# Taking every third weighted sum of the first tile's rounds from TensorE to ScalarE and GpSimd

## The reference

```python
def peer_block(x, wq, k1, k2, U, V):
    ...
    e = (...)                                   # 8 heads x 16 experts of 16384, for each token
    g = jax.nn.softmax(sc, axis=-1)
    act = jax.nn.gelu(jnp.einsum('nd,nhjd->nhj', x, U[e]), approximate=False)
    out = jnp.einsum('nhj,nhjd->nd', g * act, V[e])
    return out.astype(x.dtype)
```

## Time and profile before

| what | value |
|---|---|
| median of 3 runs | 2743.24 us (2741.44 to 2760.86) |
| the profiled execution | 2737.79 us, its span from first to last instruction 2735.9 us |
| busy, share of the span | PE 84%, DVE 53%, ACT 15%, POOL 14% |
| mean granted TensorE clock | 0.941 of full speed |
| gathers | 320, 671.11 MB, 58.3% of the 16 DMA engines' span |
| first gather issued, last gather issued | 1027.1 us, 2704.1 us |
| time in which POOL sat idle ahead of a gather until TensorE had summed a row | 1301.0 us, 311 times |
| time in which DVE sat idle ahead of a dot until a gather had landed | 521.2 us |

### The profile page before, as it was taken

How to read it: one execution, slowest core, us unless ns; L and a number is a source line. 1 busy time by engine, 2 the same in 40 slices (tenths; PEclk the granted TensorE clock), 3 DMA queues, 4 the chain that set the end, 5 groups by cost and what they waited for, 6 DMA issues and landing times.

```text
span 2735.9 us, 21188 instructions
## 1 busy us (share of the span) xinstructions
PE 2301.7 (84%) x7673; PEld 1264.8 (46%) x7673; DVE 1458.5 (53%) x2651; ACT 417.9 (15%) x879; POOL 379.7 (14%) x363
## 2 busy tenths in 40 slices
PE   4999999785689898999899999877877777777776
PEld 3999999543555343434344444322322232222221
DVE  4333333465620015656754455888888865555554
ACT  3222222321310010011200001211111100010000
POOL 0000000000010001221212222222222122222221
PEclk8999999866589899999999999999999999999999
DMA  4444443214035879999999999999999999999997
GB/s 128 148 128 134 142 151 119 76 56 114 1 119 183 287 264 408 418 373 426 389 421 425 416 404 420 413 415 421 407 414 422 424 417 428 428 428 428 428 429 298
DMA packets 159866, 844.78 MB, mean 309 GB/s; under 512 B 9862, under 2 KB 97730, under 8 KB 117274
## 3 DMA queue, kind: packets, MB, share of 16 engines
q0 software_dynamic: 46080, 671.11, 58.3%
q1 hardware_dynamic: 113706, 172.67, 19.0%
HBM read 833.26 MB, written 10.21 MB: 308 GB/s over the span
## 4 chain that ended last, share of the span: by engine, by line
PE 56%; DMA 27%; DVE 11%; issue 4%; ACT 1%; SPq 0%; DVEq 0%; POOL 0%; ACTq 0%; POOLq 0%
DMA rows_in<-in_peer_uv,expert 26%; PE bank L246 19%; PE bank L272 7%; PE bank L1025 5%; PE bank L1026 5%; PE bank L1027 5%; PE bank L259 4%; DVE rows_in L548 3%; PE bank L1002 1%; PE bank L1217 1%; PE bank L1207 1%; PE bank L1179 1%; DVE diag L523 1%; PE bank L1143 1%; PE bank L1132 1%
## 5 line engine op out<-in xcount | busy, mean ns | idle before, releaser
L246 PE MATMUL bank<-rows_in,diag 128*128 128x512 f32 (+1 forms) x2560 | 1189.0, 611 | 268.7 <-DVE diag L523 268.1
L548 DVE CUSTOM_DVE_ANT_0 rows_in<-rows_in,x2n 128x2048 f32<-128x2048 f32 x320 | 733.5, 2292 | 521.7 <-DMA rows_in<-in_peer_uv,expert 521.2
L246 PEld LDWEIGHTS bank<-rows_in,diag 128*128 128x128 f32 (+1 forms) x2560 | 451.9, 183 | 987.3 <-issue 546.0
L454 POOL DMA_INDIRECT rows_in<-in_peer_uv,expert x320 | 364.5, 1139 | 1509.4 <-PE bank L246 1301.0
L1025 PE MATMUL bank<-xnh,wh 128*128 128x336 f32 x896 | 285.8, 319 | 23.2 <-DVE wl L1448 23.2
L356 ACT ACTIVATE dots<-dots 128x1 f32<-128x1 f32 x320 | 64.9, 203 | 1507.8 <-DVE dots L548 1507.8
L1027 PE MATMUL bank<-xnh,wl 128*128 128x336 f32 x896 | 286.0, 319 | 0.0
L1026 PE MATMUL bank<-xnl,wh 128*128 128x336 f32 x896 | 285.6, 319 | 0.0
L1448 DVE TENSOR_TENSOR wl<-wring,wh 128x2048 fp32r<-128x2048 f32 x56 | 128.2, 2292 | 266.1 <-ACT wh L1271 266.1
L1025 PEld LDWEIGHTS bank<-xnh,wh 128*128 128x128 f32 x896 | 170.6, 190 | 24.0 <-issue 24.0
L1026 PEld LDWEIGHTS bank<-xnl,wh 128*128 128x128 f32 x896 | 170.5, 190 | 0.0
(11 more groups left out here) (288 smaller groups left out, 1517.3 us busy)
## 6 DMA issues: line engine op xcount, KB each, us to landing
wring<-in_w_in SPq DMA_DIRECT2D x28, 2048.0 KB, 8.2
wk<-in_w_out SPq DMA_DIRECT2D x64, 512.0 KB, 9.1
wk<-in_peer_wq SPq DMA_DIRECT2D x64, 512.0 KB, 8.7
kT<-in_keys_t SPq DMA_DIRECT2D x16, 512.0 KB, 5.5
vpage<-in_cache_v SPq DMA_DIRECT2D x16, 512.0 KB
rows_in<-in_peer_uv,expert POOLq DMA_INDIRECT x320, 12.4
C<-in_state_C SPq DMA_DIRECT2D x4, 1024.0 KB, 5.8
out_C_sample<-C SPq DMA_DIRECT2D x4, 1024.0 KB, 4.5
```

Source lines behind the costliest of these rows:

```text
L246: mm = pe.matmul(accs[t][d][0:w, :], diag[r % ND][:, 0:w], rows_in[r % NG][:, D + 512 * d:D + 512 * d + 512], start=False, stop=(j == ROUN ...
L454: nc.gpsimd.indirect_dma_start(out=rows_in[r % NG][:], out_offset=None, in_=UV_DR, in_offset=bass.IndirectOffsetOnAxis(ap=ids[:, j:j + 1], ...
L548: nc.vector.tensor_tensor_reduce(u, u, x2n[t][:], 1.0, 0.0, ALU.mult, ALU.add, dots[t % 2][:, j:j + 1]).then_inc(S["dot_done"], 1)
```

## The change

Of tile 0's 128 rounds, those with r % 3 == 2 (2, 5, ..., 125, which are 42) no longer go through TensorE. ScalarE multiplies the dot's gelu with the gate, and then the V half of the gathered row, in place, with that number. GpSimd adds the scaled row to `h1[0]`, ahead of the gather that reuses the buffer (that of round r+4), and waits for its own add before it issues that gather. No diagonal is built for those rounds. The residual `h1[0]` now carries a part of the sum, so TensorE adds it by the identity behind tile 0's last round and not ahead of its first. VectorE signals each finished gate (`gate_ready`). The counts that stand behind `acc_done` are renumbered.

```diff
--- before.py
+++ after.py
@@ -172,6 +172,25 @@
     FIRST = [0, PH * PK, 2 * PH * PK]
     TOTAL = sum(ROUNDS)
     COLS = [P, P, TS]
+    OWN = 3
+
+    def on_pool(r):
+
+        return r < FIRST[1] and r % OWN == OWN - 1
+
+    def pool_sums(r):
+
+        return sum(1 for n in range(r) if on_pool(n))
+
+    def tensor_sums(r):
+
+        return r - pool_sums(r)
+
+    def tensor_steps(r):
+
+        return tensor_sums(r) + (1 if r >= FIRST[1] else 0)
+
+    TILE_STEPS = [tensor_sums(FIRST[1]) + 1, tensor_sums(FIRST[2]) + 1, tensor_sums(TOTAL) + 1]
 
     def tile_of(r):
 
@@ -233,19 +252,27 @@
 
             t, j = tile_of(r)
             w = COLS[t]
-            if j == 0:
+            if on_pool(r):
+                return
+            if j == 0 and t:
                 if t == 1:
                     banks_idle(pe, ("pS", 2, 3), range(4))
                 elif t == 2:
                     pe.wait_ge(S["y_done"], 1)
                 for d in range(4):
                     pe.matmul(accs[t][d][0:w, :], ident[:, 0:w], h1[t][:, 512 * d:512 * d + 512], start=True, stop=False, skip_group_check=True)
-            pe.wait_ge(S["diag_done"], r + 1)
+            n = tensor_sums(r)
+            pe.wait_ge(S["diag_done"], n + 1)
             pe.wait_ge(row_in[r % NG], 16 * (r // NG + 1))
             for d in range(4):
-                mm = pe.matmul(accs[t][d][0:w, :], diag[r % ND][:, 0:w], rows_in[r % NG][:, D + 512 * d:D + 512 * d + 512],
-                               start=False, stop=(j == ROUNDS[t] - 1), skip_group_check=True)
+                mm = pe.matmul(accs[t][d][0:w, :], diag[n % ND][:, 0:w], rows_in[r % NG][:, D + 512 * d:D + 512 * d + 512],
+                               start=(r == 0), stop=(t > 0 and j == ROUNDS[t] - 1), skip_group_check=True)
             mm.then_inc(S["acc_done"], 1)
+            if r == FIRST[1] - 1:
+                pe.wait_ge(S["own_done"], pool_sums(FIRST[1]))
+                for d in range(4):
+                    mm = pe.matmul(accs[0][d][:], ident, h1[0][:, 512 * d:512 * d + 512], start=False, stop=True, skip_group_check=True)
+                mm.then_inc(S["acc_done"], 1)
 
         def product(part, lhs, beside):
 
@@ -338,7 +365,7 @@
         def row_squares(t):
 
             w = COLS[t]
-            act.wait_ge(S["acc_done"], FIRST[t] + ROUNDS[t])
+            act.wait_ge(S["acc_done"], TILE_STEPS[t])
             for d in range(4):
                 ins = nc.scalar.activation(h1[t][0:w, 512 * d:512 * d + 512], accs[t][d][0:w, :], ACT.Square, accum_out=ssq[0:w, d:d + 1])
             ins.then_inc(S["sums_sq"], 1)
@@ -354,6 +381,12 @@
             t, j = tile_of(r)
             act.wait_ge(S["dot_done"], r + 1)
             nc.scalar.activation(dots[t % 2][:, j:j + 1], dots[t % 2][:, j:j + 1], ACT.Gelu).then_inc(S["gelu_done"], 1)
+            if on_pool(r):
+                act.wait_ge(S["gate_ready"], j // PK + 1)
+                act.wait_ge(S["gelu_done"], r + 1)
+                link(nc.scalar.mul(dots[0][:, j:j + 1], dots[0][:, j:j + 1], gate[0][:, j // PK, j % PK:j % PK + 1]))
+                v = rows_in[r % NG][:, D:2 * D]
+                nc.scalar.mul(v, v, dots[0][:, j:j + 1]).then_inc(S["scaled"], 1)
             if t and j == 0:
                 row_squares(t - 1)
             if t and j == 1:
@@ -450,7 +483,13 @@
                 if t < 2 and j % PK == 0:
                     pool.wait_ge(S["e_done"], PH * t + j // PK + 1)
                 if r >= NG:
-                    pool.wait_ge(S["acc_done"], r - NG + 1)
+                    if on_pool(r - NG):
+                        n = pool_sums(r - NG) + 1
+                        pool.wait_ge(S["scaled"], n)
+                        nc.gpsimd.tensor_tensor(h1[0][:], h1[0][:], rows_in[(r - NG) % NG][:, D:2 * D], ALU.add).then_inc(S["own_done"], 1)
+                        pool.wait_ge(S["own_done"], n)
+                    else:
+                        pool.wait_ge(S["acc_done"], tensor_steps(r - NG) + 1)
                 nc.gpsimd.indirect_dma_start(out=rows_in[r % NG][:], out_offset=None, in_=UV_DR,
                                              in_offset=bass.IndirectOffsetOnAxis(ap=ids[:, j:j + 1], axis=0)).then_inc(row_in[r % NG], 16)
 
@@ -500,7 +539,9 @@
                 nc.vector.scalar_tensor_tensor(expert[t][:, PK * h:PK * h + PK], slot[:, 0, :], float(NK), slot[:, 1, :], ALU.mult, ALU.add).then_inc(S["e_done"], 1)
                 dve.wait_ge(S["gate_exp"], PH * t + h + 1)
                 link(nc.vector.reciprocal(gsum[t][:, h:h + 1], gsum[t][:, h:h + 1]))
-                link(nc.vector.tensor_scalar(gate[t][:, h, :], gate[t][:, h, :], gsum[t][:, h:h + 1], None, ALU.mult))
+                ins = nc.vector.tensor_scalar(gate[t][:, h, :], gate[t][:, h, :], gsum[t][:, h:h + 1], None, ALU.mult)
+                ins.then_inc(S["gate_ready"], 1)
+                dve.wait_ge(S["gate_ready"], PH * t + h + 1)
 
         def halves():
 
@@ -518,9 +559,12 @@
             weight = gate[t][:].rearrange("p h k -> p (h k)") if t < 2 else gate2[:]
             src = ident if t < 2 else ident2[:]
             dve.wait_ge(S["gelu_done"], r + 1)
-            if r >= ND:
-                dve.wait_ge(S["acc_done"], r - ND + 1)
-            nc.vector.tensor_scalar(diag[r % ND][:, 0:COLS[t]], src, dots[t % 2][:, j:j + 1], weight[:, j:j + 1], ALU.mult, ALU.mult).then_inc(S["diag_done"], 1)
+            n = tensor_sums(r)
+            if on_pool(r):
+                return
+            if n >= ND:
+                dve.wait_ge(S["acc_done"], n - ND + 1 + (1 if n - ND >= tensor_sums(FIRST[1]) else 0))
+            nc.vector.tensor_scalar(diag[n % ND][:, 0:COLS[t]], src, dots[t % 2][:, j:j + 1], weight[:, j:j + 1], ALU.mult, ALU.mult).then_inc(S["diag_done"], 1)
 
         def row_mean(t):
 
@@ -807,7 +851,7 @@
             "qpad_zero", "qpad_done", "k_in0", "k_in1", "v_in0", "v_in1", "logitS_done", "expS_done", "probS_done",
             "best_done", "gate_exp", "e_done", "wk_used", "xr_in", "g2_in", "keys_in", "norm_sq", "norm_ms", "norm_rms",
             "x2n_done", "mix_dup", "c_rows",
-            "dot_done", "gelu_done", "diag_done", "acc_done", "sums_sq", "sums_ms", "sums_rms", "y_done", "gf_in",
+            "own_done", "scaled", "gate_ready", "dot_done", "gelu_done", "diag_done", "acc_done", "sums_sq", "sums_ms", "sums_rms", "y_done", "gf_in",
         )}
 
         row_in = [sem(f"row_in{n}") for n in range(NG)]
```

## The result

The changed kernel takes 2800.34 us (median of 4 runs, 2795.64 to 2805.65). The four runs of the kernel before that were taken beside it have a median of 2751.87 us, 48 us less. The ratio is 1.0187, with a 95% interval of 1.0154 to 1.022: clearly slower, by 1.5 to 2.2%. I had forecast 2739 us with a range of 2720 to 2768. The ratio of e2_write_only leaves out one of its ten executions, which took 10798 us for no known reason, where the others took 2734 to 2754.

A forecast was written before the change was run, and what follows sets the result against it. DMA and PE were both taken to bound tile 0's rounds beside the projections, DMA alone from 1700 on. Two shallower dips gave -2.6 - 1.5 = -4.1, so 2743.2 - 4 = 2739 us, range 2720 to 2768.

The forecast's parts named there:

- The bound: Tile 0's rounds beside the projections: PE 17.2 us and DMA 17.1 us for three rounds and two k-steps, both bounding.
- the ceiling: From 1050 to 1700, at most what DMA loses at 411 GB/s against 428: 26 us.
- my 4.1: Forecast gain in tile 0's rounds: 2.6 us from the first dip and 1.5 us from the second.
- The first dip: DMA share low from 1180 to 1192: gather 27 issued at 1178.8, not 1186.8; 2 of 4.6 us idle stay.
- The scaling: ScalarE's multiplication of the gathered row, priced at 1.91 us as the cast of 128 x 2048.
- The addition: GpSimd's addition of 128 x 2048, priced at 4.3 us from a copy of 64 columns, between 1.8 and 8.5.
- The step that failed: Row behind a GpSimd row: its dot starts 3.5 us late, so it needs 10.2 us, still inside 13.2.
- The 6.7: A TensorE row's time from landing to next issue: dot, gelu, diagonal and round, 6.7 us.
- my terms: A TensorE row's parts: 2.29 + 0.1 (dot), 0.2 (gelu), 0.3 + 0.4 (diagonal), 3.43 (round).
- a limit of 13.2: Four buffers at 5.7 us a round give 22.9 us; less 9.7 for a gather, 13.2 from landing to issue.
- The addition is slow and holds the next dot: Rival, row behind a GpSimd row: additions from 7.3 us on exceed 13.2; at 8.5, +48 us, 2791; chance 0.14.
- its rival: TensorE's clock falls with gaps in its work, deciding only from 0.80 down; at 0.75, +46 us, 2789; chance 0.08.

The follow-up runs named there:

- e2_write_only: Changed kernel with each GpSimd addition replaced by two memsets of the used buffer: 759.3 us from gather 0 to gather 136 (the stage), ratio to before 1.000.
- e13_no_add_late_dot: Changed kernel without GpSimd's additions, VectorE reducing 3500 columns ahead of 32 dots behind GpSimd rows: 794.9 us from gather 0 to gather 136, ratio to before 1.0113.

## Why the prediction was wrong

**The bound and the ceiling held.** DMA and TensorE both bound the stage. TensorE's saving brought nothing by itself; with the additions taken away the stage gained 4.5 us (7.5 without scaling) against my 4.1 and a ceiling of 26. That 4.5 and 4.1 are so near is luck: 11 us were gained, of which I had 4.1, and 7 lost, of which I had none.

**The first dip went as described.** In the changed kernel gather 27 is issued 25.7 us behind gather 23, where it was 33.1; I had 25.1. Without additions it is 22.0 us, and gather 28 follows 37.4 us behind gather 23 (33.3 in the changed kernel) against 36.2 forecast. The dip is shallower; stretches of the run without additions:

```profile
1201.00:1207.00 6.00, 6.00 (x16) 2.65 (x15) 4.13 (x9) 2.50 (x3) 0.89 (x1) 1.00 0.79 314
1207.00:1213.00 6.00, 6.00 (x16) 2.65 (x15) 3.68 (x11) 0.20 (x1) 1.93 (x3) 1.00 0.88 344
```

That is (0.21 + 0.12) x 6 = 2.0 us idle, where the earlier trace rows give 4.6. I had said that 2 us would stay.

**The prices.** The scaling: 1.91 forecast, 2.00 measured. The addition: 4.3 forecast, 4.54 on average (4.50 undisturbed). The figure of the Trainium skill, 4497 ns (GPSIMD Engine Reference, section 3.1), was nearer. The row that my price came from, a copy of 64 columns, was a poor ground: a long copy takes 1.89 us, so my slope was twice too steep, and it came out near the truth by luck, as an addition takes over twice as long as a copy.

**The step that failed** is "If GpSimd and VectorE shut each other out, that dot starts 3.5 us late and its row needs 6.7 + 3.5 = 10.2 us, still inside 13.2." The exclusion was foreseen, with its place and its size (115 us over 31 dots, 3.7 each). What was wrong is the row's path around it and the slack that I tested it against: a delay of 3.8 us alone, with GpSimd doing nothing but issue gathers, already cost 35 us in e13_no_add_late_dot. The 6.7 was too small from the start. From the end of a dot to the gather into its buffer my terms have 0.2 + 0.3 + 0.4 + 3.43 = 4.3 us. In the timelines it is, on average over the 36 rows behind a GpSimd row from round 12 to round 119, 7.9 us in the kernel before, 6.6 without additions and 8.1 in the changed kernel. There these rows take 13.8 us on average from landing to issue, and up to 21.5, where I had 10.2 against a limit of 13.2.

One row shows the terms. The one that lands at 1455.9 has its dot until 1462.0 (6.1 us, 5.9 by my terms), the diagonal until 1462.7, then TensorE's round, which I had at 3.43. It takes 8.85 - 3.43 = 5.4 us: TensorE had been idle for 5 us, and its clock was granted at 0.68 and 0.76 in these microseconds; then 0.26 for the hand-over. The gather into this buffer is issued at 1468.4, 12.5 us after the landing, and its issue takes 2.49 and not 0.94 us, as it waits for the next dot. The effective time is 12.5 + 1.55 = 14.1 us against 13.2. Two smaller errors go the same way. The 13.2 us were for rounds of 5.7 us; with the projections gone a round is due each 4.9, the loop is 19.6 us, and the margin shrinks by 3.3 us: there each addition cost 2.3 us in place of 1.1. And I tested each buffer alone against its limit, when the delay of one dot is handed to the row behind it, which waits for the same VectorE and the same TensorE. How much of the loss each of these terms makes is not shown; no run takes one of them away alone. The slow issues aren't needed for it: the run with late dots has only 26 of 132 over 1.5 us (25 before) and lost 35 us.

**The rival.** "The addition is slow and holds the next dot" was the right mechanism with a wrong threshold. I let it decide from 7.3 us on, and it decides between 2.35 and 4.5 us (768.0 and 818.3 us in the stage). My 48 us for it were near the measured 54 by luck, for an addition of 8.5 us. TensorE's clock fell from 0.99 to 0.90 as its rival had it, and didn't decide by itself: at 0.93 the run without additions lost nothing over the stage. It has a part in the slow restart above; how much of the loss that is, and whether it makes the 7 us that this run loses behind gather 104, stays open.

## What to carry to other kernels

In these runs VectorE and GpSimd behaved as one engine wherever both read SBUF. So before work is moved to the idle one of the two, look at what the other does in the same microseconds, and price the mover's whole length as a delay of it, on dots, diagonals and short helpers alike. When such a delay is checked against the slack of a ring of buffers, read the path itself from the trace and don't add it up from its parts, add the terms that only appear once things are late (a matmul that starts after idleness, an issue that waits in its turn), and take the ring's shortest period, not its usual one. And ask first what can be won: here 42 rows taken away for almost nothing brought 7.5 us of 2740.

## What the runs showed of the hardware that I had not expected

- The exclusion works in both directions: an addition that comes just behind a dot's start takes 6.6 us in place of 4.5. And it works on the issue of an indirect DMA: 0.94 us undisturbed, 2.7 us beside a dot, ending 0.8 us after it. With VectorE's long sums 60 of the first 132 issues took over 1.5 us, and in the kernel before already 25.
- A GpSimd copy with one input holds dots back as an addition does (dots of up to 4.70 us); GpSimd memsets don't, but they hold the diagonals, a `tensor_scalar` of 128 columns, which then take up to 4.1 us in place of 0.35.
- Cutting GpSimd's instruction in four doesn't let VectorE in between each time: one instruction of 0.42 us took 5.66.
- GpSimd writes 0.86 ns for each column in a memset, takes 0.92 for a copy and 2.2 for an addition.
- The same instructions ahead of the first gather took 1027 to 1033 us in eight of the 16 traces and 1042 to 1045 us in the other eight, with nothing between. The cause is not shown.
